# The modulation's matrix products moved from TensorE to GpSimd and VectorE, with the first layers' fillers reordered

## What is computed

```python
    c_act = jax.nn.silu(c)
    for i in range(DEPTH):
        mod = c_act @ ada_w[i] + ada_b[i]      # 1024 x 6144
        sh1, sc1, g1, sh2, sc2, g2 = jnp.split(mod[:, None, :], 6, axis=-1)
        h = x * (1 + sc1) + sh1
        ...
        x = layer_norm(DEEPNORM_ALPHA * x + (1 + g1) * y, ln_g[i, 0], ln_b[i, 0])
        h = x * (1 + sc2) + sh2
        ...
```

## Time and profile before

| | |
|---|---|
| median of 3 runs | 1768.91 us |
| profiled execution: its time, its span | 1769.17 us, 1767.4 us |
| TensorE busy | 1568.4 us, 89% |
| VectorE, ScalarE, GpSimd busy | 376.5, 215.7 and 107.3 us |
| layer 0 | 18.6 to 217.1 us |
| layer 1 | 217.1 to 421.0 us |
| transposes mT and qkv projection | 421.0 to 518.6 us |
| neighbourhood attention | 518.6 to 603.5 us |
| DMA | 534 MB, mean 302 GB/s |

### The profile page before, as it was taken

One profiled execution on the slowest core, in us unless ns is written; L12 is line 12 of the kernel. 1 busy time (PEld: TensorE's weight loads), 2 busy tenths in 40 slices (PEclk: granted clock), 3 DMA queues, 4 the chain that ended last, 5 costly groups with the idle time before them and its releaser, 6 DMA issues.

```text
span 1767.4 us, 28139 instructions
## 1 busy us (share of the span) xinstructions
PE 1568.4 (89%) x12784; PEld 941.0 (53%) x12784; DVE 376.5 (21%) x971; ACT 215.7 (12%) x579; POOL 107.3 (6%) x109
## 2 busy tenths in 40 slices
PE   6999999987999789998898889689899988988984
PEld 3454445454846557554564555257465646545641
DVE  1411223111013240111011101354321110111113
ACT  2221113110014211000000000124110000000000
POOL 3102010020000020000000000210200000000001
PEclk9999999988998679999998999898899989989998
DMA  9447645563458447999999999932379999999994
GB/s 350 159 143 246 237 167 190 196 233 120 143 176 319 171 166 323 382 427 426 426 425 428 427 426 410 331 143 88 143 315 380 429 426 426 425 429 426 426 419 172
DMA packets 96889, 534.38 MB, mean 302 GB/s; under 512 B 5088, under 2 KB 7296, under 8 KB 73200
## 3 DMA queue, kind: packets, MB, share of 16 engines
q1 hardware_dynamic: 92992, 519.40, 73.3%
q0 software_dynamic: 3760, 13.00, 1.9%
HBM read 531.32 MB, written 1.05 MB: 301 GB/s over the span
## 4 chain that ended last, share of the span: by engine, by line
PE 67%; DMA 20%; DVE 5%; ACT 3%; issue 2%; SPq 1%; POOL 1%; DVEq 0%; ACTq 0%; POOLq 0%
PE bk L378 30%; DMA AR<-in_moe_w_down 19%; PE bk L768 17%; PE bk L800 7%; PE bk L810 3%; ACT AR L1590 3%; PE bk L374 3%; PE bk L414 2%; DVE AR L883 2%; PE bk L432 2%; SPq L2042 1%; PE bk L591 1%; DMA ring<-in_w_in 1%; POOL st L1906 1%; DVE sm L894 1%
## 5 line engine op out<-in xcount | busy, mean ns | idle before, releaser
L378 PE MATMUL bk<-ring,AR 128*128 128x512 f32 (+2 forms) x896 | 381.7, 585 | 15.6 <-DMA ring<-in_w_in 7.9
L768 PE MATMUL bk<-ring,AR 128*32 128x128 f32 x5120 | 307.3, 409 | 0.0
L378 PEld LDWEIGHTS bk<-ring,AR 128*128 128x128 f32 x896 | 172.6, 195 | 214.1 <-issue 200.4
L768 PEld LDWEIGHTS bk<-ring,AR 128*32 128x32 f32 x5120 | 193.2, 127 | 96.9 <-DVE AR L883 4.6
L768 PE MATMUL bk<-AR 128*32 128x128 f32 x3072 | 187.0, 409 | 0.0
L1590 ACT ACTIVATE AR<-bk 128x128 f32<-128x128 f32 (+4 forms) x147 | 60.4, 426 | 996.9 <-PE bk L768 765.8
L800 PE MATMUL bk<-AR 128*32 128x512 f32 x368 | 141.3, 679 | 45.2 <-DMA AR<-in_moe_w_down 44.5
L768 PEld LDWEIGHTS bk<-AR 128*32 128x32 f32 x3072 | 125.5, 128 | 53.8 <-DVE AR L883 4.6
L800 PE MATMUL bk<-ring,AR 128*32 128x512 f32 x656 | 148.4, 693 | 5.3 <-DMA ring<-in_moe_w_down 5.2
L883 DVE TENSOR_TENSOR AR<-bk,AR 128x128 f32<-128x128 f32 (+1 forms) x72 | 24.2, 336 | 510.0 <-ACT AR L1590 466.9
L378 PE MATMUL bk<-AR,X 128*128 128x128 f32 x512 | 124.5, 412 | 0.2
(11 more groups left out here) (138 smaller groups left out, 961.0 us busy)
## 6 DMA issues: line engine op xcount, KB each, us to landing
ring<-in_moe_w_gate SPq DMA_DIRECT2D x48, 2048.0 KB, 24.1
ring<-in_moe_w_down SPq DMA_DIRECT2D x36, 2048.0 KB, 28.8
ring<-in_moe_w_up SPq DMA_DIRECT2D x32, 2048.0 KB, 20.3
AR<-in_moe_w_up SPq DMA_DIRECT2D x32, 2048.0 KB, 29.0
ring<-in_ada_w SPq DMA_DIRECT2D x24, 2048.0 KB, 10.3
AR<-in_moe_w_down SPq DMA_DIRECT2D x20, 2048.0 KB, 28.3
AR<-in_moe_w_gate SPq DMA_DIRECT2D x16, 2048.0 KB, 16.4
ring<-in_w_in SPq DMA_DIRECT2D x12, 2048.0 KB, 8.9
```

The source lines that it names most:

```text
L378: ins = eng.matmul(o, l, r, start=i == 0, stop=i == len(pairs) - 1)
L768: ins = eng.matmul(o[32 * f:32 * f + 32, 128 * m:128 * m + 128], XG[u][:, c, 32 * j:32 * j + 32], w[:, c, f::4], start=c == 0, stop=c == N ...
```

## The change

GpSimd computes pieces 0 to 12, six in layer 0 and seven in layer 1: column chunk by column chunk it multiplies the weights, in the ring slot itself, by c (a scalar for each partition) and adds the result to `mpart`. VectorE computes pieces 13 to 23 in the qkv projection of the neighbourhood block, with one scaled addition a chunk. TensorE only sums over the partitions: `total()` is one product of a 128 x 128 matrix of ones with `mpart`, for each of the 24 pieces, twelve in the first layers (table entry `tot`, and one behind the output projection), one ahead of the qkv projection, ten behind its products (`NA_TOTALS`) and one in the attention. Its result has the same row in every partition; VectorE's `extract()` takes the gates from one row, and for a shift or scale multiplies by the identity and reduces, which gives the column.

`FILL` is regrouped into one tuple of entries a step; the spatial gate's norm moves ahead and is cut in two (`svar`, `svn`), the gate's silus are in two halves (`gates`, semaphores `gsil1`, `gsil`), loads have a table of their own (`LOADS`, `NA_LOADS`), and nothing is left in the attention of the second block but one sum. In the neighbourhood block `norm_columns` moves behind the scaling of mT. `cbc`, `sel`'s use and ScalarE's `ada_part` are gone. Lines in after's code are shifted: what was L374, L378, L591, L1902, L1906, L1944 and L2042 is L379, L383, L569, L1885, L1889, L1954 and L2057.

```diff
-FILL = (("qk0", "qk1", "v0", "v1", "ada", "a0", "ada", "a1", "b0", "b1", "g0", "g1", "ada", "s0", "s1", "ada",
-         "pre", "ada", "conv", "ada", "spat", "ada", "ada", "ada"),
-        ("qk0", "qk1", "v0", "v1", "ada", "a0", "a1", "ada", "b0", "b1", "ada", "ada", "g0", "g1", "ada", "ada",
-         "s0", "s1", "pre", "ada", "conv", "spat", "ada"))
...
+FILL = ((("qk0",), ("qk1",), ("v0",), ("v1", "tot"), ("s0",), ("s1", "tot"),
+         ("a0", "svar"), ("a1", "tot", "svn"), ("b0",), ("b1",), ("g0", "tot"), ("g1", "gates"), ("conv",), ("spat",)),
+        (("qk0", "tot"), ("qk1", "tot"), ("v0",), ("v1", "tot"), ("s0",), ("s1", "tot"),
+         ("a0", "svar"), ("a1", "tot", "svn"), ("b0",), ("b1",), ("g0", "tot"), ("g1", "gates"), ("conv",), ("spat",)))
+LOADS = (("cq", "qk", "v", "ada", "s", "ada", "a", "ada", "b", "ada", "g", "ada", 0, "ada", 1),
+         ("cq", "qk", "ada", "v", "ada", "s", "ada", "a", "ada", "b", "ada", "g", 0, "ada", 1, "ada"))
+NA_LOADS = (0, "ada", 1, "ada", 2, "ada", 3, "ada", 4, "ada", 5, "ada", "ada", "ada", "ada", "ada", "ada")
+POOL_ADA = 13
+NA_STEPS = (1, 1, 2, 2, 2, 2)
+NA_TOTALS = (1, 2, 1, 2, 2, 2)
...
+            def total():
+                i, j = divmod(n_tot[0], 12)
+                n_tot[0] += 1
+                o = begin(next_bank(), "adaT", i, j)
+                pe.wait_ge(sem("ones"), 1)
+                if n_tot[0] <= POOL_ADA:
+                    pe.wait_ge(sem("ada"), n_tot[0])
                 else:
-                    rv = mpart[:, :].rearrange("p (k c) -> p c k", c=8)
-                    for c in range(8):
-                        ins = eng.matmul(o[:, c:c + 1], rv[:, c, :], sel[:, 0:1], start=True, stop=True)
-                end(ins, "adaT", i, j)
+                    pe.wait_ge(sem("adav"), n_tot[0] - POOL_ADA)
+                end(product(o[:, :], [(ones[:, :], mpart[:, 512 * (j % 2):512 * (j % 2) + 512])]), "adaT", i, j)
...
+                        if f == "tot":
+                            total()
...
                 pe.wait_ge(*drained("out", 1, 1, 1))
                 columns(X, "mT", 0)
                 wait_columns("mT", 0)
+                fill_bank[0] = [2, 3]
+                total()
                 for j in range(6):
                     w = piece(("qkv", 0, j), NC, 512)
                     pe.wait_ge(*loaded("qkv", 0, j))
...
                             ins = product(o[:, :], [(HT[:, c, u * 128:(u + 1) * 128], w[:, c, :]) for c in range(NC)])
                         end(ins, "qkv", 0, j, u)
                     DONE["qkv", 0, j] = filled("qkv", 0, j, 1)
+                    for k in range(NA_TOTALS[j]):
+                        total()
...
+            def ada():
+                n = n_ada[0]
                 n_ada[0] += 1
+                i, j = divmod(n, 12)
+                acc = mpart[:, 512 * (j % 2):512 * (j % 2) + 512]
+                w = piece(("ada", i, j), NC, 512)
+                v.wait_ge(sem("silc"), 1)
+                v.wait_ge(*loaded("ada", i, j))
+                v.wait_ge(*filled("adaT", *divmod(n - 2, 12)))
+                v.step(ts(acc, w[:, 0, :], ccol[:, 0:1], ALU.mult))
+                for c in range(1, NC):
+                    v.chain()
+                    ins = stt(acc, w[:, c, :], ccol[:, c:c + 1], acc, ALU.mult, ALU.add)
+                    if c < NC - 1:
+                        v.step(ins)
+                DONE["ada", i, j] = v.tell(ins, sem("adav"), n + 1 - POOL_ADA)
...
+            def extract():
+                i, j = divmod(n_tot[0], 12)
+                n_tot[0] += 1
                 k, hf = divmod(j, 2)
-                if not (hf or k in (2, 5)):
-                    return
                 v.wait_ge(sem("in2"), 16 * (8 + DEPTH))
                 v.wait_ge(*filled("adaT", i, j))
                 if k in (2, 5):
                     r = 32 * (2 * i + k // 3)
                     o = grow[r:r + 1, 512 * hf:512 * hf + 512]
                     free(stt(o, bank("adaT", i, j)[r:r + 1, :], 1.0, o, ALU.add, ALU.add), "adaT", i, j)
-                else:
-                    free(stt(mod[:, i, 8 * k:8 * k + 8], bank("adaT", i, j)[:, 0:8], 1.0 if k in (1, 4) else 0.0,
-                             abc[:, i, 8 * k:8 * k + 8], ALU.add, ALU.add), "adaT", i, j)
-            def last_ada():
-                i, j = divmod(n_ada[0] - 1, 12)
-                while not (j % 2 or j // 2 in (2, 5)):
-                    j -= 1
-                return drained("adaT", i, j)
+                    return
+                h = slice(64 * hf, 64 * hf + 64)
+                own = diag[h, :].rearrange("p (k c) -> p k c", c=8)
+                free(tt(own, bank("adaT", i, j)[h, :].rearrange("p (k c) -> p k c", c=8), bcast(ident[h, h], 2, 8), ALU.mult),
+                     "adaT", i, j)
+                v.chain()
+                v.step(red(dsum[h, :], own.rearrange("p k c -> p c k"), ALU.add))
+                if hf:
+                    v.chain()
+                    v.tell(stt(mod[:, i, 8 * k:8 * k + 8], dsum[:, :], 1.0 if k in (1, 4) else 0.0,
+                               abc[:, i, 8 * k:8 * k + 8], ALU.add, ALU.add), sem("mod"), 4 * i + (0, 1, 2, 3)[k - k // 3] + 1)
...
+                    for f in todo.pop(0) if todo else ():
+                        if f in work:
+                            work[f]()
...
-                norm_columns(0, 0, 3)
...
+                extract()
+                norm_columns(0, 0, 3)
+                ada()
+                extract()
...
                     free(ts(d, o, 0.125, ALU.mult) if j < 2 else eng.tensor_copy(d, o), "qkv", 0, j, 0)
-                first = [True]
+                    for k in range(NA_TOTALS[j - 1] if j else 0):
+                        extract()
+                    for k in range(NA_STEPS[j]):
+                        ada()
+                for k in range(NA_TOTALS[5]):
+                    extract()
...
+            def ada(steps):
+                for _ in range(steps):
+                    n, c = divmod(n_ada[0], NC)
+                    n_ada[0] += 1
+                    i, j = divmod(n, 12)
+                    acc = mpart[:, 512 * (j % 2):512 * (j % 2) + 512]
+                    w = piece(("ada", i, j), NC, 512)[:, c, :]
+                    if not c:
+                        g.wait_ge(sem("silc"), 1)
+                        g.wait_ge(*loaded("ada", i, j))
+                        if n > 1:
+                            g.wait_ge(*filled("adaT", *divmod(n - 2, 12)))
+                        g.step(eng.tensor_scalar(acc, w, ccol[:, 0:1], None, ALU.mult))
+                        continue
+                    g.step(eng.tensor_scalar(w, w, ccol[:, c:c + 1], None, ALU.mult))
+                    g.chain()
+                    ins = tt(acc, acc, w, ALU.add)
+                    if c < NC - 1:
+                        g.step(ins)
+                    else:
+                        DONE["ada", i, j] = g.tell(ins, sem("ada"), n + 1)
...
                 rsqrt(st2[:, 48:50], st[:, 32:34], "xrs", l + 1)
+                if l:
+                    ada(8)
                 g.wait_ge(sem(f"lay{l}"), 64)
                 for k in range(4):
                     ins = eng.affine_select(out=sgw[:, k, :], in_=sgw[:, k, :], compare_op=ALU.is_ge, fill=0.0, base=0,
...
                         g.step(ins)
                 g.wait_ge(sem("var6"), l + 1)
                 rsqrt(st2[:, 0:6], st[:, 0:6], "rs6", l + 1)
+                ada(8)
                 g.wait_ge(sem("var8"), l + 1)
                 rsqrt(st2[:, 32:48], st[:, 8:24], "rs8", l + 1)
+                ada(8)
                 g.wait_ge(sem("var12"), l + 1)
                 rsqrt(st2[:, 8:24], st[:, 40:56], "rs12", l + 1)
-                for seg in ("v", "a", "b", "g", "s"):
+                ada(8)
+                g.wait_ge(sem("svar"), l + 1)
+                rsqrt(st2[:, 24:26], st[:, 60:62], "srs", l + 1)
+                svv = sect(SV, 256)
+                g.wait_ge(sem("svn"), l + 1)
+                g.step(tt(svv, svv, rowb(R_LG, 256), ALU.mult))
+                g.chain()
+                g.tell(tt(svv, svv, rowb(R_LB, 256), ALU.add), sem("sgv"), l + 1)
+                ada(8)
+                for seg in ("a", "b"):
                     for t in range(NT):
                         g.wait_ge(*drained("in", l, seg, t))
                 g.wait_ge(sem("moba"), l + 1)
...
                         g.tell(ins, sem("taps"), l + 1)
                     else:
                         g.step(ins)
-                g.wait_ge(sem("svar"), l + 1)
-                rsqrt(st2[:, 24:26], st[:, 60:62], "srs", l + 1)
-                svv = sect(SV, 256)
-                g.wait_ge(sem("svn"), l + 1)
-                g.step(tt(svv, svv, rowb(R_LG, 256), ALU.mult))
-                g.chain()
-                g.tell(tt(svv, svv, rowb(R_LB, 256), ALU.add), sem("sgv"), l + 1)
-                g.wait_ge(sem("gsil"), l + 1)
+                g.wait_ge(sem("gsil1"), l + 1)
```

(1 more changed line is left out.)

276 lines of the change are left out of this document (103 added, 173 removed).

## The result

| | before | after |
|---|---|---|
| median (runs) | 1769.0 us (1768.3 to 1769.4) | 1830.8 us (1827.2 to 1834.1) |
| profiled execution | 1769.2 us | 1831.6 us |
| ratio after/before | | 1.0349, 95% interval 1.0329 to 1.037 |
| forecast | | 1746.6 us, range 1715 to 1780 |

What follows compares the result with a forecast made beforehand. TensorE's list of work was taken to bound the first layers. First layers -39.2 and neighbourhood stage +16.9 gave -22.3 us from 1769.2: 1746.9 profiled, 1746.6 us as median, range 1715 to 1780.

Steps and rivals of the forecast that it cites:

- GpSimd's piece: First layers: eight scalings at 0.6 us and seven additions at 1.27 us make a piece of 13.7 us.
- rival C: GpSimd's scaling is dear and rsqrts behind pieces become the bound: 1768 us at 1.27, 1784 at 1.6; chance 0.22.
- the prediction's own sign of being wrong: First layers: wrong if GpSimd is still in a piece when VectorE calls for rs8 or rs12.
- Waits behind a piece: First layers: rs8 and rs12 follow a piece each; the first is done at 49, ahead of VectorE's call at 54.1.
- Holding: First layers: VectorE stands still beside GpSimd's pieces, 12.3 us in the MLA chain and 7.9 in the MoBA chain.
- Extraction in VectorE's order: First layers: twelve sums priced at 0.93 us each on TensorE, with no VectorE cost for extracting them.
- Work left on TensorE in the first layers: 378.3 us less the modulation's products, sums and a toll, plus 11.2 us of new sums: 314.2 us.
- the 7.8 us toll: First layers: slower w_in chunks behind the one-column sums, 2.3 us in layer 0 and 5.5 in layer 1, gone.
- 3.0 us a layer: First layers: allowance for TensorE's clock falling after the new waits, 3.0 us in each layer.
- Three stalls in the projection: Neighbourhood projection: loads wait for products 3, 4 and 5, and TensorE's sums wait for them, 14.1 us each.
- Attention at the grouped one's pace: Neighbourhood attention without modulation: the grouped attention's 40.2 us plus 2.6 for bias additions, 43 us.

Runs made afterwards that it cites:

- e3: The changed kernel with GpSimd's scaling written as a product of two inputs, the column repeated along the row: 1843.7 us.
- e1: The changed kernel with one scaling for each of GpSimd's 13 pieces, seven of eight terms left out: 1793.2 us.
- e11: The kernel of e1 with the two sums among each first layer's attention entries moved behind the attention: 1769.1 us.
- e5: The kernel before with only the eight one-column sums replaced by one 128x512 product for each half: 1766.4 us, ratio 0.9977.
- e4: The changed kernel with another order of loads, VectorE steps and sums in the neighbourhood projection, extraction ahead of eviction: 1776.9 us.
- e12: The kernel of e4 with eight products that nobody reads added in each of the neighbourhood attention's ten steps: 1772.6 us.
- e10: The kernel of e1 with eight products that nobody reads ahead of each of eight entries in either first layer's attention: 1825.5 us.
- e2: The changed kernel with GpSimd's 13 pieces replaced by memsets that read nothing: 1851.8 us.
- e7: The kernel of e4 with only the first two of the neighbourhood attention's eight bias tiles loaded: 1775.7 us.
- e6: The kernel of e5 with the last seven pieces on VectorE in the neighbourhood projection and the norm's constants waited for behind the scaling: 1732.5 us, ratio 0.9746.

## Why the prediction was wrong

The forecast was 84 us too low. Of these, 53 lie in the first layers, 21 in the neighbourhood attention and 9 in the projection.

- **GpSimd's piece: wrong, and the step that failed first.** "I take 0.6, between 0.29 and 1.27 (no slower than two inputs)": the scaling takes 1.56, outside both bounds, and a piece 21.9, not 13.7. affine_select's 0.29 us for 128 columns said nothing of the scaling, and one input is not cheaper than two; e3 even has the two-input form at 1.04. The 769 ns quoted under rival C are half of it too. GpSimd was still in a piece when VectorE called for rs8 and rs12, the prediction's own sign of being wrong. e1 puts all of GpSimd's cost at 37.6 us, 31.7 of it in the first layers. Rival C had the right side and, with the late inverse roots, half the mechanism; its price for 1.6 us, 1784, was 47 too low.
- **Waits behind a piece: partly missed.** rs8 and rs12 late was C's; a piece ahead of layer 1's rs6 (11.6 us on TensorE), the last one ahead of the projection's first sum (5.8) and the norm's constants, whose DMAs GpSimd issued at 442.8 behind its last piece, were in no sum.
- **Holding: too dear in the change.** 12.3 and 7.9 us forecast, 3.6 and 2.1 measured, where only GpSimd's additions hold; 14.2 and 12.1 in e3, where every operation has two inputs.
- **Extraction in VectorE's order: put at nothing.** I costed a sum in the first layers at 0.93 us of TensorE and nothing on VectorE. In the attention it holds up the softmax step behind it: 24 us (e11 against e1), as much as the forecast gain.
- **Work left on TensorE in the first layers: 314.2 us forecast, 345.8 measured.** The sums cost what I had (12.6 for 11.2 us). But the 7.8 us toll, which e5 shows can be had back, was not won: waits took its place ahead of the chunks, and the rest of the list took 22.5 us longer than before. For the clock I had put 3.0 us a layer. Much of this belongs to the two points above, since in e11, without either, the same work takes 329.2. That e11's first layers take 361.3 us, where I had 363.2, is luck: 15 us more work, 17 us less waiting, and GpSimd's part, which the forecast did contain, left out.
- **Three stalls in the projection: right**, 14.5 us against 14.1. e4 gets 54 us back.
- **Attention at the grouped one's pace, 43 us: wrong,** 64.3. The grouped attention's 40.2 us were at a granted clock of 0.88, and I had read 0.79 for this one with the modulation in it and left the clock out. Of the 21 us, 17 are TensorE's busy time, 52.6 us against the grouped attention's 35.6, and e12 shows that the clock sets it. The old 82.7 us held 29 us of modulation work that cost 18.

The profile's chain of work that ended last agrees: TensorE's share of it falls from 67 to 48%, GpSimd's rises from 1 to 13%.

## What to carry to other kernels

Before work goes to an idle engine, list what else stands in that engine's queue, and time the exact operation on it: its neighbours in the table can be off by more than a factor of two, and the form decides whether it holds VectorE. Work that fills TensorE's waits can be nearly free, since it also keeps the clock (e12, but not e10); taking it away then wins less than its busy time (18 of 29 us here). And where a ring is shared, look for a consumer one step behind a load whose slot the step just ahead frees.

## What the runs showed of the chip

- On GpSimd a 128x512 scaling by a column takes 1.56 us, the same product with the column repeated as a second input 1.04, an addition of two full inputs 1.27, a memset 0.52.
- Two-input GpSimd operations of 128x512 hold VectorE's two-input operations to their end (19.8 us for a chain of 5.6, e3); the scaling by a column lets them pass and takes up to 2.35 us itself; memsets hold nothing (5.9 us, e2). The 128x16 power of the earlier trace rows has two inputs as well and held nothing. Why is open.
- In the neighbourhood attention TensorE ran at half its clock even while its records followed one another without a gap (576.83 to 593.38 in e7), and with 19 us of idle work added it ran at the full one from 577.6 on (e12). What sets the level was not tried further.
- Runs of one kernel vary more in e4 to e12 than the kernel before did at first (e6 from 1719.8 to 1742.4, the kernel before beside e11 and e12 from 1767.3 to 1784.3). The part from the neighbourhood attention's output projection on took 1157 us in the profiled e5 and 1171 in e6, with the same instructions. Why is open.
- Not tried: GpSimd's pieces with buffers of their own, so that all sums could wait for the end of the attention.
